# A shared first modulation, an earlier folding and a compression in four column groups, in a two-block transformer kernel on one Trainium2 core

## What is computed

```python
c_act = silu(c)
mod = c_act @ w_ada[l] + b_ada[l]            # six vectors of 1024: shift, scale, gate, twice
h = rms_norm(x, g_pre_mix[l]) * (1 + sc_mix) + sh_mix
u = h @ w_in[l]                              # x_m, z, glu_a, glu_b
x_c = silu(causal_depthwise_conv(x_m, w_conv_m, b_conv_m))      # 4 taps
q, k = x_c @ w_q, x_c @ w_k                  # per head
v = x_m @ w_v
gates = concat(q, k, v) @ w_gates + b_gates
a = causal_depthwise_conv(glu_a * sigmoid(glu_b), w_dw, b_dw)   # 31 taps
```

## Time and profile before

| | |
|---|---|
| median of 3 runs | 2027.92 us (2026.99 to 2028.9) |
| profiled execution | 2027.99 us |
| its span | 2026.2 us, 20909 instructions |
| mean granted PE clock | 0.985 |
| PE | 1866.7 us busy, 92% |
| PE weight loads | 1381.0 us, 68% |
| DVE | 1056.6 us, 52% |
| ACT | 505.3 us, 25% |
| POOL | 323.8 us, 16% |
| DMA | 517.39 MB, mean 255 GB/s |

### The profile page before, as it was taken

One profiled execution on the slowest core, in us unless ns is written; L12 is line 12 of the kernel. 1 busy time (PEld: TensorE's weight loads), 2 busy tenths in 40 slices (PEclk: granted clock), 3 DMA queues, 4 the chain that ended last, 5 costly groups with the idle time before them and its releaser, 6 DMA issues.

```text
span 2026.2 us, 20909 instructions
## 1 busy us (share of the span) xinstructions
PE 1866.7 (92%) x8020; PEld 1381.0 (68%) x8020; DVE 1056.6 (52%) x2575; ACT 505.3 (25%) x1226; POOL 323.8 (16%) x341
## 2 busy tenths in 40 slices
PE   6999999999999999999999999998888887887777
PEld 5877788888887788888888787885343342443332
DVE  6996665401797422001201432236867677767755
ACT  2043221111214222110012545121322222222223
POOL 1000001000000000000000000013443444444441
PEclk9999999999999999999999999999999999998999
DMA  9614469844352143449552323529999999999996
GB/s 397 262 55 159 186 253 422 343 157 150 134 209 81 64 182 134 159 153 208 218 199 99 116 101 117 216 110 422 421 421 421 421 421 421 421 421 422 420 421 277
DMA packets 72435, 517.39 MB, mean 255 GB/s; under 512 B 8208, under 2 KB 8464, under 8 KB 11664
## 3 DMA queue, kind: packets, MB, share of 16 engines
q0 software_dynamic: 46384, 330.85, 40.7%
q1 hardware_dynamic: 25952, 185.21, 24.1%
HBM read 510.78 MB, written 5.24 MB: 255 GB/s over the span
## 4 chain that ended last, share of the span: by engine, by line
PE 57%; DMA 20%; DVE 18%; ACT 3%; issue 1%; POOL 1%; DVEq 0%; SPq 0%; POOLq 0%; ACTq 0%
DMA region<-in_peer_uv,small 18%; PE pj L624 12%; PE pj L887 10%; PE pj L902 9%; DVE region L1713 9%; PE st L1170 6%; PE pj L830 5%; DVE region L2125 2%; PE pj L637 2%; PE pj L931 1%; PE pj L1141 1%; DMA ring<-in_ring_w 1%; PE st L1089 1%; PE ms L830 1%; PE pj L922 1%
## 5 line engine op out<-in xcount | busy, mean ns | idle before, releaser
L1170 PE MATMUL st<-region 128*128 128x512 f32 x940 | 453.3, 631 | 111.5 <-ACT region L1549 111.5
L1170 PEld LDWEIGHTS st<-region 128*128 128x128 f32 x940 | 182.3, 200 | 361.7 <-issue 189.3
L624 PE MATMUL pj<-hT,ring 128*128 128x256 f32 x1760 | 385.0, 380 | 1.0 <-ACT region L1353 1.0
L2125 DVE CUSTOM_DVE_ANT_0 region<-region 128x1024 f32<-128x1024 f32 x235 | 287.3, 1224 | 163.7 <-DMA region<-in_peer_uv,small 161.3
L624 PEld LDWEIGHTS pj<-hT,ring 128*128 128x128 f32 x1760 | 332.6, 190 | 47.1 <-ACT region L1353 1.8
L528 POOL DMA_INDIRECT region<-in_peer_uv,small x235 | 259.4, 1104 | 393.6 <-PE st L1170 322.4
L887 PE MATMUL pj<-region,ring 128*128 128x256 f32 x1024 | 222.0, 379 | 0.5 <-DMA ring<-in_ring_w 0.5
L887 PEld LDWEIGHTS pj<-region,ring 128*128 128x128 f32 x1024 | 194.3, 190 | 28.0 <-DMA ring<-in_ring_w 0.9
L1549 ACT ACTIVATE region<-ident,small 128x128 f32<-128x128 f32 x256 | 89.2, 394 | 456.1 <-DVE small L2133 456.1
L1713 DVE SCALAR_TENSOR_TENSOR region<-region,pc 128x255 f32<-128x255 f32 (+19 forms) x528 | 202.6, 462 | 0.0
L1664 DVE TENSOR_TENSOR tmp<-xT,hT 128x256 f32<-128x256 f32 x32 | 13.6, 425 | 359.1 <-ACT hT L1249 359.1
(11 more groups left out here) (382 smaller groups left out, 1987.0 us busy)
## 6 DMA issues: line engine op xcount, KB each, us to landing
ring<-in_ring_w SPq DMA_DIRECT2D x157, 1024.0 KB, 4.8
region<-in_ada_rest POOLq DMA_DIRECT2D x40, 1024.0 KB, 12.4
region<-in_ada_first SPq DMA_DIRECT2D x8, 1024.0 KB, 18.6
region<-in_wqkv SPq DMA_DIRECT2D x2, 3072.0 KB, 12.1
region<-in_wcmp POOLq DMA_DIRECT2D x2, 2048.0 KB, 9.9
bias_dram<-region POOLq DMA_DIRECT2D x1, 4096.0 KB, 46.0
region<-in_w_o POOLq DMA_DIRECT2D x4, 1024.0 KB, 7.1
region<-in_peer_uv,small POOLq DMA_INDIRECT x235, 17.0
```

What stands on the lines that cost most here:

```text
L624: i = nc.tensor.matmul(b[:, m, :], w[:, k, P * m:P * m + P], hT[:, k, :], start=(k == 0), stop=(k == CT - 1))
L1170: i = nc.tensor.matmul(acc[:, u % 2, 512 * hf:512 * hf + 512], diag[:, m % NDIAG, :], uv[m % NBUF][:, D + 512 * hf:D + 512 * hf + 512], st ...
L2125: nc.vector.tensor_tensor_reduce(row, row, h_tok[:, u % 2, :], 1.0, 0.0, ALU.mult, ALU.add, dots[:, u, k:k + 1]).then_inc(sem("u_used"), 1)
```

## The change

Three edits, with their consequences:

1. Of the first eight modulation pairs, the scale half of pairs 3 to 7 (`SHARED = 3`) is no longer reduced by DVE. POOL multiplies it by c_act, ACT sums the product with a copy that accumulates, and DVE waits for that sum before `first_h(c)`. ACT does the sum of pair c+1 before it finishes tile c.
2. The folding of w_v into w_gates of layer 0 is done by PE before `wide_first`. wvT goes into the w_q part of wqkv, loaded with wg right behind the parameter columns; the load of wqkv waits for the folds. PE's column sums of the squares move behind w_in job 4, where they replace the filler, write to st, and are reduced by DVE between the row chain and the last five taps. Layer 1 keeps its order.
3. The compression alternates even and odd positions i_ between two column groups for each m, four in all. ACT copies four pieces to cmp_rows (128 partitions now, cleared by a DVE memset); four matmuls with columns of the identity turn the rows and add even and odd.

```diff
-EARLY = ["ada0", "x", "ada1", "cols", "ada2", "ring", "ada3", "ring", "ada4", "ada5", "ada6", "ada7", "ring", "ring"]
+SHARED = 3
+EARLY = ["ada0", "x", "ada1", "cols", "wv", "ada2", "ring", "ada3", "ring", "ada4", "ada5", "ada6", "ada7", "ring", "ring"]
...
-        wvT = tmp[:, :, :]
+        wvT = [wqkv[:, 0], tmp[:, :, :]]
...
-        cmp_rows = small_piece(3072, P, 64)
+        cmp_rows = small_piece(3072, P)
...
+                elif what == "wv":
+                    sp.dma_start(wvT[0], a["wvT"][0].rearrange("p (c d) -> p c d", d=DH)).then_inc(sem("wg_in"), 16)
+                    sp.dma_start(wg[:, :, :], a["wg"][0]).then_inc(sem("wg_in"), 16)
...
                 if l:
                     sp.wait_ge(sem("head_done"), H * l)
+                else:
+                    sp.wait_ge(sem("wvg_made"), 1)
                 sp.dma_start(wqkv[:, :, :, :], a["wqkv"][l]).then_inc(sem("wqkv_in"), 16)
...
-            pool.wait_ge(sem(f"ada_first{PAIRS - 1}"), 16)
+            pool.wait_ge(sem("c_ready"), 1)
+            for j in range(SHARED, PAIRS):
+                pool.wait_ge(sem(f"ada_first{j}"), 16)
+                nc.gpsimd.tensor_tensor(ada_first[:, j, 1, :], ada_first[:, j, 1, :], c_act, ALU.mult).then_inc(sem("c_and_products"), 1)
...
-            for s in range(2):
-                for c in range(CT):
-                    i = nc.tensor.matmul(ms[0][:, 0, CT * s + c:CT * s + c + WIDE], tmp[:, c, P * s:P * s + P], ones[:, 0:WIDE], start=True, stop=True)
-            i.then_inc(sem("x_summed"), 1)
...
                 if l == 0:
+                    for c in range(2 * H):
+                        fold_gates(l, c)
                     wide_first(W_IN_ORDER[:2])
...
                         wide_tile(("w_in", l, j), m, b)
-                        fold_gates(4 * n + 2 * m)
-                        fold_gates(4 * n + 2 * m + 1)
+                        if l:
+                            fold_gates(l, 4 * n + 2 * m)
+                            fold_gates(l, 4 * n + 2 * m + 1)
...
                     wide("w_in", l, [4])
-                    keep_awake(st[:, 0, :], 6)
+                    for s in range(2):
+                        for c in range(CT):
+                            i = nc.tensor.matmul(st[:, 0, CT * s + c:CT * s + c + WIDE], tmp[:, c, P * s:P * s + P], ones[:, 0:WIDE], start=True, stop=True)
+                    i.then_inc(sem("x_summed"), 1)
...
-                    i = nc.tensor.matmul(ms[1][32 * m:32 * m + 2 * NCMP, 0, 0:P], blk[:, m, :, :, i_], wcmp[m][:, i_, :],
-                                         start=(i_ == 0), stop=(i_ == CMP_LEN - 1))
+                    q = 64 * m + 32 * (i_ % 2)
+                    i = nc.tensor.matmul(ms[1][q:q + 2 * NCMP, 0, 0:P], blk[:, m, :, :, i_], wcmp[m][:, i_, :],
+                                         start=(i_ < 2), stop=(i_ >= CMP_LEN - 2))
...
-                        lo, hi = 32 * n, 32 * n + 2 * NCMP
-                        t = nc.tensor.transpose(ms[1 - n][:, 0, lo:hi], cmp_rows[lo:hi, :], ident[lo:hi, lo:hi])
+                        for lo in (64 * n, 64 * n + 32):
+                            t = nc.tensor.matmul(ms[1 - n][:, 0, 0:2 * NCMP], cmp_rows[64 * n:64 * n + 64, :], ident[64 * n:64 * n + 64, lo:lo + 2 * NCMP],
+                                                 start=(lo == 64 * n), stop=(lo > 64 * n))
...
+                    if l == 0 and shift == 0 and SHARED <= c + 1 < CT:
+                        act.wait_ge(sem("c_and_products"), 16 + c + 2 - SHARED)
+                        nc.scalar.activation(ada_first[:, c + 1, 1, :], ada_first[:, c + 1, 1, :], ACT.Copy,
+                                             accum_out=mod_sum[:, PAIRS + c + 1:PAIRS + c + 2]).then_inc(sem("x_and_sums"), 1)
                     act.wait_ge(sem("h_scaled"), h_tiles)
...
                 finish_h(l, 0)
                 if l == 0:
+                    keep_fold(l)
...
-            for n in range(2):
-                i = nc.scalar.copy(cmp_rows[32 * n:32 * n + 2 * NCMP, :], ms[1][32 * n:32 * n + 2 * NCMP, 0, 0:P])
+            for q in range(0, P, 32):
+                i = nc.scalar.copy(cmp_rows[q:q + 2 * NCMP, :], ms[1][q:q + 2 * NCMP, 0, 0:P])
...
                 dve.wait_ge(sem(f"ada_first{j}"), 16)
-                for m in range(2):
+                for m in range(1 if j >= SHARED else 2):
                     ada_tile(ada_first[:, j, m, :], PAIRS * m + j)
...
+                if c >= SHARED:
+                    dve.wait_ge(sem("x_and_sums"), 16 + c - SHARED + 1)
+                    dve.sem_inc(sem("ada_used"), 1)
+                    ada_at += 1
...
-            dve.wait_ge(sem("x_summed"), 2)
-            invs += 1
-            link_to(nc.vector.tensor_reduce(x_sum, ms[0][:, 0, 0:2 * CT].rearrange("p (s c) -> p s c", c=CT), AX.X, ALU.add), "x_sum_kept", invs)
...
                 if l == 0:
+                    dve.wait_ge(sem("x_summed"), 2)
+                    invs += 1
+                    link_to(nc.vector.tensor_reduce(x_sum, st[:, 0, 0:2 * CT].rearrange("p (s c) -> p s c", c=CT), AX.X, ALU.add), "x_sum_kept", invs)
                     long_conv(l, 3, range(KC - 5, KC))
...
             dve.wait_ge(sem("params2_in"), 32)
+            nc.vector.memset(cmp_rows, 0.0)
```

47 lines of the change are left out of this document (25 added, 22 removed).

## The result

The changed kernel takes 2035.55 us (median of 6 runs, 2034.09 to 2036.22), the kernel before 2028.91 on the same chip: a ratio of 1.0037, 95% interval 1.0027 to 1.0047. It is slower by about 6.6 us. The forecast was 2032.6 (slower by over 0.2% with 53%), its range ended at 2035.2, 0.35 us too early. The profiled execution took 2034.09 us, the shortest of the six, 6.1 above the profiled execution of before.

The account below looks back on a forecast made before the run. The prediction took the start to be bound by DVE, never idle from 42.98 to 150.95 us. Start +6.4, column sums +1.2 and compression -2.9 gave +4.7, 2032.6 us, range 2027.4 to 2035.2.

Parts of the forecast that it names:

- The start: Modulation pairs 3 to 7: DVE and POOL take turns, so the last hT tile and first convolution come later, +6.4 us.
- one odd 1.01 us on POOL: POOL's one-column select at 8.26 us, read as POOL waiting for DVE's two-input instruction to end; others took 0.3.
- the first rival: At the start, no exclusion between DVE and POOL: start costs 1.6 us, total -0.1, 2027.8 us; chance 17%.
- My walk: Start, step by step from pair landings: 4 DVE sums (4.6), small operations (3.4), 4 products (8.8), one after another, 16.8 us.
- Part 1: Early loads of wvT and wg ahead of the third pair: 2.7 us of transfer, nearly no cost to DVE's old order.
- The folding: Folds moved ahead of the first projection, while PE waits for tile 0: 0; PE's 3.2 us saved in layer 0 uncounted.
- Part 4: Column sums behind w_in tile 4: DVE's row part 2.7 us later, 1.6 of slack used, +1.2 us left at head 0.
- The compression: Four column groups for two, -3.5 us, and longer turning back, +0.6; -2.9 us in all, PE being the chain.
- The rival of strided weights: Compression: strided weight loads set 0.056 us per record, so four groups gain nothing, 2036.1 us; chance 8%.
- the second: Rival at the start: a short POOL product of 1.05 us with exclusion, start +2.0, 2028.2 us; chance 10%.
- PE sets layer 0 after all: Rival: folding's 3.2 us come off the path, with a cheap start, 2024.1 us or below; chance 5%.
- The clock: PE's granted clock falling after idle time before tiles 2 and 4 at the start; up to 1 us reaches the end; 5%.

Follow-up runs that it names:

- experiment 3: The changed kernel with the column sums moved into the gap where layer 0's folds had stood, and the fillers back behind w_in tile 4: 2031.72 us, ratio 1.0018.
- experiment 8: The changed kernel with DVE's last five taps of head 3 ahead of its wait for and reduction of the column sums: 2036.04 us, ratio 1.0042.
- experiment 9: The changed kernel with three 256-column filler matmuls set between the column sums: 2033.98 us, ratio 1.0028.
- experiment 5: The changed kernel with POOL's five products replaced by memsets that read nothing, product with c left out: 2029.69 us, ratio 1.0007.
- experiment 6: The changed kernel with POOL's five products each replaced by two one-input copies and a short memset, product with c left out: 2032.84 us, ratio 1.0023.
- Experiment 7: The kernel before with only wvT and wg also loaded ahead of the third modulation pair, unread there: 2030.14 us, ratio 1.0012.
- experiment 10: The changed kernel with sharing off and the column sums in the gap, fillers back, leaving early loads, early folding and compression: 2026.42 us, ratio 0.9993.
- experiment 2: The changed kernel with SHARED = 8, so DVE does all its modulation sums and POOL's loop is empty: 2029.98 us, ratio 1.001.
- experiment 12: The changed kernel with four filler matmuls on PE ahead of its waits for hT tiles 3, 4 and 5: 2034.66 us, ratio 1.0035.
- experiment 1: The kernel before with only the compression in four column groups: 2024.5 us, ratio 0.9985.
- experiment 11: The kernel before with the four-group compression and three fillers instead of six behind w_in tile 4: 2024.83 us, ratio 0.9985.
- experiment 4: The kernel before with the six fillers behind w_in tile 4 replaced by twelve unread 48-column matmuls: 2028.33 us, ratio 1.0002.

## Why the prediction was right in direction and short in size

**The start, forecast +6.4, measured +6.26 in the profiled execution.** The mechanism is right; that the number is met to 0.2 us is in part luck, since experiments 3, 8 and 9, with the same start, show 8.0, 9.0 and 7.7. In medians the start costs 6.3 to 7.2 us (below). The first convolution was to come at 49.4 and came at 49.24, the last hT tile to be scaled at 46.1 and it was at 45.90. The reading of one odd 1.01 us on POOL carried it, and experiments 5 and 6 confirm what it stood for: a two-input instruction of DVE and an instruction of POOL that reads SBUF run one at a time. The rule in the Trainium skill (SBUF — State Buffer, Who interferes with whom), named in the prediction against the first rival, agrees: the small operations of 1.00, 2.27 and 2.53 us and the memset run say the same from both sides. The product took 2.35 us alone, against 2.2 taken; the estimate of 2.25 by the Trainium skill (GPSIMD Engine Reference, section 3.1, Elementwise) lies 0.1 under it. My walk counted all small operations of DVE at full length. In truth those of tile 4 fell where one product gave way to the next, and DVE did the sums of pairs 5 to 7 after the last product. So the last four products took 9.3 us and not 8.8, the small operations 3.0 and not 3.4, and the total came out because the two errors cancel.

**The remark on the loads was wrong by itself.** Part 1 says they "would cost nearly nothing to DVE's old order". Experiment 7 shows +2.4 at the first convolution and 1.8 at the end. I compared pair 3's landing (23.9) with when DVE took it (23.57), and the last pair's (36.3) with 36.38, but not pair 4's, 28.9 against 26.78. From there on DVE works without a pause to the end of the start, so 2.1 us of waiting at pair 4 are never recovered; a landing on time for the last pair says nothing. In the sum this was hidden, because the walk of part 2 started from the landings.

**The folding, forecast 0.** At the start no cost is seen: the first convolution is 2.37 us late in experiment 10 and 2.39 in 7, which lacks the folding. (The folds took 4.32 us and not 3.5, and the clock was at 1.2 GHz from 19.8 to 26.6 behind them, off the path.) Around 110 us the forecast held in the change's own execution: PE's offset falls to 3.8 us at 121.8 and is back to 6.3 at q's second head. But PE now stands idle there for 3.0 us where it was 0.5, and I had not asked what the clock makes of that. In three of the seven profiled executions with this gap empty (experiments 2, 8 and 12) it fell between 126.9 and 132.4, for 0.9 to 2.2 us on PE; in the seven others, with the folds or the sums in the gap, it did not.

**The column sums, forecast +1.2, measured +4.1. This is the step that failed.** Part 4 says "The slack of 1.6 us is used up and +1.2 us is left". Its reckoning on DVE was right (2.4 us of delay there for 2.7, and 1.6 of slack). But PE is the later one: +0.9 us by the sums' length, then 3.3 us more, since its granted clock was at 1.2 GHz for 6.8 us from 159.7: the turning and the four records of L770 and L771 by 0.5, the scores 2.93 us for 1.57, L627 5.08 for 3.62. I had named the clock once, for PE's idle time at the start, and had not asked it of the edit that takes out matmuls called `keep_awake`. The evidence that the narrow matmuls in this place did it: of the six profiled executions of kernels with the bare sums behind tile 4 (the change, experiments 2, 5, 6, 8, 12) five show a fall between 155.8 and 162.8 us; of the seven with 256-column fillers there or between the sums (before, 1, 3, 7, 9, 10, 11) none does, and experiment 4 brings it about in the kernel before. The cost goes with the length of the fall: from the sums' start to the numerators PE loses 4.2 us where it lasts 6.8 (the change, 5 and 6), 2.6 where it lasts 3.4 (2 and 12) and 0.9 without it (8). In medians moving the sums to the gap wins 2.7 us (change against experiment 3) to 3.7 (experiment 2 against 10), and that holds what the filled gap saves as well.

The shape alone is not enough, and what else is needed stays open. The same 32 records of 48 columns stand at 16 to 21 us in the kernel before and in experiments 1, 4 and 11, and in the gap in experiments 3 and 10, and no fall follows in any of the six. Behind tile 4 they are followed by the turning, a wait of 0.26 us and four-row matmuls; in those six wide matmuls come within 0.4 us. In experiment 7, where the sums at 17 to 20 us are followed by a wait of 1.5 us, the clock falls at 22.1. No run tests whether what comes next is the reason.

**The compression, forecast -2.9, measured -3.05.** 3.75 us for 3.6 forecast, turning back 0.64 for 0.9. Experiment 1 gives -3.3 at the end. The rival of strided weights falls.

**The sum.** Counted from the kernel before on the same chip, the change costs +6.6 us against +4.7 forecast, and the forecast range reached to +7.3; so 1.0 us of the miss in absolute time is that before itself took 2028.91 there and not 2027.92. The parts, in medians over before: compression -3.3 (experiment 1), loads +1.8 (7), sums +2.7 to 3.7, sharing +4.5 (change against 2) to 5.4 (experiment 3 against 10). The low price of the sums belongs to the high one of sharing, and the other way round, so the parts make 6.6 or 6.7 for 6.6 measured; what is tested in that is only that loads and compression add up to experiment 10. With the sums at the forecast's 1.2 it would be 4.2 to 5.1. The parts don't reach the end to better than a microsecond: from 1366 to 1396 us the offsets of these kernels shift by up to 1.8 us, though they do the same work there.

**The rivals.** DVE's stretched rows rule out the first rival, and products of 2.35 us the second; "PE sets layer 0 after all" fell where it was put, at 110 us. PE does set the heads at 160, where no rival stood. The clock had 5% and was looked for at the start alone.
